# The row sums of the token norms from two rounded halves, and those of the second block one strip later

## What is computed

```python
def _rms_norm(x, g):
    xf = x.astype(jnp.float32)
    y = xf * lax.rsqrt(jnp.mean(xf * xf, axis=-1, keepdims=True) + EPS)
    return (y * g.astype(jnp.float32)).astype(x.dtype)
...
        h = h + mixed @ w_out[l]
        h = h + _cross_attention(_rms_norm(h, norm_x_g[l]), _rms_norm(mem, norm_mem_g[l]),
                                 xa_wq[l], xa_wk[l], xa_wv[l], xa_wo[l])
        h = h + jnp.square(jax.nn.relu(_rms_norm(h, norm_ff_g[l]) @ ff_w1[l])) @ ff_w2[l]
    return _rms_norm(h, final_norm_g)
...
        # second block, on that result
        h = rmsnorm(x, ln1_g[l])
        proj = h @ w_in[l]
        b_a, c_a, x_a, x_b, g_b, gate_a_logit, gate_b_logit = jnp.split(proj, SPLIT_POINTS, axis=-1)
        y_a = b_a * causal_depthwise_conv(c_a * x_a, conv_a_w[l])
        u_b = causal_depthwise_conv(x_b, conv_b_w[l], conv_b_b[l])
        y_b = rg_lru(u_b, lru_wa[l], lru_ba[l], lru_wx[l], lru_bx[l], lru_lambda[l])
...
        h = rmsnorm(x, ln2_g[l])
        x = x + (jax.nn.silu(h @ w_ffn_gate[l]) * (h @ w_ffn_up[l])) @ w_ffn_down[l]
```

## Time and profile before

| | |
|---|---|
| Time, median of 3 runs (lowest to highest) | 1694.38 us (1694.36 to 1695.56) |
| The profiled execution: time, span of the trace | 1695.03 us, 1693.2 us |
| Busy in the span: TensorE | 1660.7 us (98%), 7450 matmul records |
| VectorE, ScalarE, GpSimd | 894.1, 645.5, 823.7 us |
| Granted TensorE clock, mean | 0.995 of full |
| Plain fp32 matmul records of the token norms (L679 and L1165) | 8 and 2, 0.59 us each |
| Waits of TensorE for GpSimd's low parts (L570) | 6.9 us in 3 waits, one of them 6.2 us |

### The profile page before, as it was taken

The page is one execution under the profiler, slowest core; times in us unless marked ns, Lnnn a source line. Parts: engine busy times, 40 slices in busy tenths (PEclk is TensorE's granted clock), DMA queues, the critical chain, the costliest instruction groups (busy, mean ns, idle before and its releaser), DMA issues.

```text
span 1693.2 us, 21197 instructions
## 1 busy us (share of the span) xinstructions
PE 1660.7 (98%) x7450; PEld 1361.5 (80%) x7450; DVE 894.1 (53%) x1176; ACT 645.5 (38%) x827; POOL 823.7 (49%) x604
## 2 busy tenths in 40 slices
PE   7989999999999999999999999999999999999997
PEld 5868878888778888888888888888888888888886
DVE  7997896664357333344557676743333432232234
ACT  5534334443233221122345657563333431222222
POOL 4555245645225444444436656564444444444443
PEclk9999999999999999999999999999999999999999
DMA  6113222243112233223223333332233222222323
GB/s 238 62 63 100 87 66 97 88 150 99 62 63 89 98 99 99 94 92 99 99 87 114 110 101 119 103 105 93 99 99 99 88 99 99 97 90 98 99 99 100
DMA packets 48927, 167.04 MB, mean 99 GB/s; under 512 B 5285, under 2 KB 7461, under 8 KB 48618
## 3 DMA queue, kind: packets, MB, share of 16 engines
q1 hardware_dynamic: 44864, 158.51, 28.2%
q10 hardware_dynamic: 4010, 7.80, 1.3%
HBM read 164.18 MB, written 2.11 MB: 98 GB/s over the span
## 4 chain that ended last, share of the span: by engine, by line
PE 47%; issue 20%; POOL 14%; DVE 1%; DMA 0%; ACT 0%; POOLq 0%; DVEq 0%; SPq 0%
PE ps L651 16%; PE ps L653 16%; PE ps L652 16%; POOL m_w_lo L570 13%; DMA m_raw<-in_strips 0%; POOL m_QL L611 0%; DVE m_h L2584 0%; PE ps L910 0%; PE ps L912 0%; PE ps L911 0%; ACT m_w_hi L1253 0%; POOLq L587 0%; POOLq L585 0%; DVE ps L2170 0%; DVE m_s L2161 0%
## 5 line engine op out<-in xcount | busy, mean ns | idle before, releaser
L570 POOL TENSOR_TENSOR m_w_lo<-m_raw,m_w_hi 128x512 fp32r<-128x512 f32 x582 | 791.7, 1382 | 812.4 <-ACT m_w_hi L1253 812.2
L1253 ACT ACTIVATE m_w_hi<-m_raw 128x1024 fp32r<-128x1024 f32 x291 | 306.8, 1057 | 590.4 <-DMA m_raw<-in_strips 590.3
L651 PE MATMUL ps<-m_XH,m_w_hi 128*128 128x512 f32 x1096 | 437.6, 399 | 7.3 <-POOL m_w_lo L570 6.9
L653 PE MATMUL ps<-m_XH,m_w_lo 128*128 128x512 f32 x1096 | 427.7, 390 | 0.0
L652 PE MATMUL ps<-m_XL,m_w_hi 128*128 128x512 f32 x1000 | 390.0, 390 | 0.0
L651 PEld LDWEIGHTS ps<-m_XH,m_w_hi 128*128 128x128 f32 x1096 | 206.4, 188 | 57.7 <-POOL m_w_lo L570 9.8
L653 PEld LDWEIGHTS ps<-m_XH,m_w_lo 128*128 128x128 f32 x1096 | 206.1, 188 | 43.4
L652 PEld LDWEIGHTS ps<-m_XL,m_w_hi 128*128 128x128 f32 x1000 | 188.3, 188 | 41.9 <-issue 4.1
L651 PE MATMUL ps<-m_FH,m_w_hi 128*128 128x512 f32 (+1 forms) x438 | 169.3, 387 | 0.3 <-DVE m_FL L1791 0.3
L653 PE MATMUL ps<-m_FH,m_w_lo 128*128 128x512 f32 (+1 forms) x438 | 169.1, 386 | 0.0
L652 PE MATMUL ps<-m_FL,m_w_hi 128*128 128x512 f32 (+1 forms) x438 | 169.1, 386 | 0.0
(11 more groups left out here) (410 smaller groups left out, 2198.8 us busy)
## 6 DMA issues: line engine op xcount, KB each, us to landing
m_raw<-in_strips SPq DMA_DIRECT2D x294, 512.0 KB, 3.3
m_x_in<-in_x SPq DMA_DIRECT2D x4, 512.0 KB, 8.1
m_spread<-g_kept ACTq DMA_DIRECT2D x8, 256.0 KB, 3.3
m_x_res<-in_x ACTq DMA_DIRECT2D x1, 2048.0 KB, 9.2
m_memf<-in_mem SPq DMA_DIRECT2D x1, 1024.0 KB, 14.6
m_w<-in_w ACTq DMA_DIRECT2D x2, 512.0 KB, 8.6
m_decay<-in_decay ACTq DMA_DIRECT2D x1, 1024.0 KB, 11.8
out<-m_h SPq DMA_DIRECT2D x8, 128.0 KB, 1.7
```

The source lines that it names most:

```text
L570: nc.gpsimd.tensor_tensor(w_lo[:, c], raw[:, c], f(w_hi[:, c]), ALU.subtract).then_inc(lo_ready, 1)
L651: pe.matmul(dst, hi[:, c], xh, start=first, stop=False)
L653: return pe.matmul(dst, lo[:, c], xh, start=False, stop=last)
L1253: act.activation(w_hi[:, c], raw[:, c], ACT.Copy).then_inc(hi_ready, 1)
```

## The change

Every norm's row sum is now made from two rounded parts. VectorE splits the sum of squares into a high part (rounded to fp32r) and the rest, two instructions (`split`), where it only raised a semaphore before. TensorE multiplies a block of ones in fp32r by each part into one bank, two matmuls of 512 columns (`rows_sum`) in place of a plain fp32 one. The ones in fp32r lie where `tri[0]` was and are written once, in the first block, behind the use of the mask. The high and low part of `acc` lie in `s0` and `s1`, those of `e0` in `e1` and, in place, in `e0`. In the second block both row sums move from behind the strip w = 0 to behind the strip w = 1 of turn 0.

```diff
+        ones_r = at("ones_r", P, small + 256 + (NCOL + 2 * P) * 4, F32R)
+        acc_hi = at("acc_hi", T, small + 9760, F32R)
+        acc_lo = at("acc_lo", T, small + 11808, F32R)
+        e_hi = at("e_hi", T, 192 * KB + 5632, F32R)
+        e_lo = at("e_lo", T, 192 * KB + 3584, F32R)
...
             def norm(n):
                 pe.wait_ge(norm_sum, n)
-                pe.matmul(ps[:, 7, :], ones, acc[:], start=True, stop=True).then_inc(norm_all, 1)
+                rows_sum(7, acc_hi, acc_lo).then_inc(norm_all, 1)
+
+            def rows_sum(bank, hi, lo):
+
+                pe.matmul(ps[:, bank, :], ones_r[:], hi[:], start=True, stop=False)
+                return pe.matmul(ps[:, bank, :], ones_r[:], lo[:], start=False, stop=True)
...
-                        if first and w == 0:
+                        if first and w == 1:
                             norm(4)
-                            pe.matmul(ps[:, 6, :], ones, e0[:], start=True, stop=True).then_inc(norm_two, 1)
+                            pe.wait_ge(norm_sum, 5)
+                            rows_sum(6, e_hi, e_lo).then_inc(norm_two, 1)
...
                         if u == 0:
-                            norm(5)
+                            norm(6)
...
             def mlstm_sums():
 
                 ch.sync()
+                ch.add(dve.tensor_copy(ones_r[:], ones))
                 dve.wait_ge(m_sums, 4 * TT)
...
                 dve.wait_ge(summed, 8 * r + KT)
-                dve.sem_inc(norm_sum, 1)
+                split(acc_hi[:], acc_lo[:], acc[:], 1.0, norm_sum)
...
             dve.wait_ge(summed, 16 + KT)
+            split(acc_hi[:], acc_lo[:], acc[:], 1.0, norm_sum)
             dve.wait_ge(summed_two, KT)
-            dve.sem_inc(norm_sum, 1)
+            split(e_hi[:], e_lo[:], e0[:], 1.0, norm_sum)
             dve.wait_ge(norm_all, 5)
```

## The result

After the change the kernel takes **1698.85 us** (median of 19 runs, 1697.06 to 1701.19), against 1695.56 us for the kernel before in the same comparison (19 runs, 1694.36 to 1696.91). The ratio is 1.0020 with an interval of 1.0013 to 1.0026: 3.3 us slower, 0.2%, small but clear of noise by the interval, where 3.5 were forecast. The profiled execution took 1698.85 us, its span is 1697.1 us.

The account below looks back on a forecast made before the run. In the second block's turns the chain of VectorE and ScalarE was taken to lead, TensorE following without slack. A 4.84 us late chain less 1.34 us from rounded sums gave +3.5 us on 1694.38: 1697.9 us, range 1696.6 to 1700.0.

Parts of the forecast that it names:

- The rounded sum: Norms 2, 3 and 5 on TensorE's path: 0.45 us less each, 1.34 us gained, at least 1.20.
- The splits: VectorE's two instructions ahead of each sum, 1.2 to 3.2 us: hidden, 0; not hidden if the sum came at 875.00.
- Rival D: Splits come late at three norms, up to 0.9 us each, with GpSimd beside them: 1700.5 us; chance 2%.
- The copy of the ones: One 128x128 VectorE instruction in the first block, at most 1.3 us, covered by a 7.29 us wait: 0.
- The chain: VectorE and ScalarE's hand-offs from turn 0's moved sums start 4.84 us late (4.80 to 5.04); each later step shifts alike.
- The two waits: Turn 0: TensorE waits 3.4 us for strip S_IN + 4, then 2.7 us for the next turn's first strip; clock at 1.00.
- Rival A: TensorE's clock falls behind turn 0's new waits, 2 us each, first absorbed, second costing 0 to 2: 1698.9 us; chance 10%.
- Turn 1: Second block: turn 1 begins 4.84 us late, whatever TensorE saved in turn 0; less than 4 would refute the argument.
- The turns: Second block: turns stay 28.87 us, TensorE's own work 28.56; the 0.3 us are waits for the chain, with no catching up.
- rival B: The chain catches up in the turns, TensorE pays only the S_IN + 4 wait: +1.2 us, 1695.6 us; chance 8%.
- Rival C: Late sums cost nothing if S_IN + 4's high part is ready regardless: -2.2 us, 1692.1 us; chance 6%.
- The sum: Whole kernel: 4.84 late less 1.34 gained, +3.5 us, 3.4 to 3.9: 1697.9 us, 0.21% slower.

Follow-up runs that it names:

- r_first: The changed kernel with the second block's row sums put back behind the strip w = 0, rounded sums kept: 1695.34 us, ratio 1.0002.
- r_second_high: The changed kernel with ScalarE's high part of strip S_IN + 4 taken ahead of its two roots in turn 0: 1697.78 us, ratio 1.0018.
- r_second_defer: The changed kernel with the final norm's two VectorE steps and root made later in turn 0, off the way to `pX`: 1695.70 us, ratio 1.0001.
- the three kernels with the swap: Next turn's `pX` taken before the BH/BL split, in the kernel before, with rounded sums behind w = 0, and in the changed kernel: 0.9996, 0.9993, 1.0015.
- r_second_defer_swap_mg: The changed kernel plus deferred second norm, `pX` ahead of the BH/BL split, and the merge's fourth strip's high part earlier: 1694.43 us, ratio 0.9994.
- r_first_early: The changed kernel, sums back behind w = 0, with ScalarE taking the high part of each next turn's first strip one step earlier: 1697.87 us, 1.0017.
- r_first_swap: The changed kernel, sums back behind w = 0, with the next turn's `pX` taken ahead of the BH/BL split: ratio 0.9993.

## Why the prediction was right

**The rounded sum: right.** Forecast 0.45 us each, at least 0.40; measured 0.43 at norms 2 and 3, about 0.5 at norm 5 in `after` and 0.4 in `r_first`. Sum forecast 1.34, measured 0.86 + 0.51 = 1.37 in `after`, 1.25 in `r_first`.

**The splits: hidden at every norm**, as the median of the earlier trace rows had it. Rival D is out. The one split that met a low part beside it (1.66 us at 874.28) ended at 875.94, 4.1 us ahead of the sum. The sentence that it wouldn't be hidden at 875.00 is shown by `r_first`: 0.78 us of wait there.

**The copy of the ones** took 1.28 us, the upper end of its bound, and cost nothing: VectorE still waited 6.05 us for TensorE behind it. The cover was what counted.

**The chain: 4.84 us late, to the hundredth.** VectorE's first step came 6.11 us behind w = 0 (forecast 6.1), the second sum's wait of 0.24 us went, `pX` and the high part of S_IN + 4 are 4.85 and 4.84 late. Every step behind kept its length nearly.

**The two waits: in place, both smaller.** 3.15 us for 3.4, and 1.24 for 2.7. The first is short by 0.25, since TensorE reached it nearly 0.1 later and the low part came 0.16 earlier than worked out. The second is short by what the clock took in between, 1.63 us, less those 0.16. **This is the one statement on the mechanism that failed**: the granted clock was to stay at 1.00 behind both waits, and was 0.53 behind the first. The mistake was to take the wait of 2.41 us that had not lowered it for a guide to one of 3.4. The same trace has a shorter one, of 2.27 us, that did lower it; timeline of TensorE and the clock behind it, of the kernel before:

```profile
254.87 3.99 PE L845 MATMUL ps<-m_VX,m_W 128*128 128x129 f32 x20 [2.27 <-DVE m_acc L2076]
```

```profile
254.87:258.87 4.00, 4.00 (x21) 4.00 (x22) 1.84 (x3) 1.06 (x1) 2.06 (x2) 0.59 0.06 22
```

Rival A named the case, with 2 us behind the first wait that only eat into the second; that is what happened, and so the time didn't change. By the prediction's own sign ("if the clock falls, it is A") the case is A, and the 1698.85 us measured are A's 1698.9 and not the forecast's 1697.9. But A's number holds 1 us for its other half, a slow clock behind the second wait, which didn't come in `after`; the agreement with it is luck, as this section's last paragraph shows. `r_second_high` and `r_second_defer` did run into a low clock in front of turn 1, and lost 1.95 and 1.38 us between C and D, within A's range of 0 to 2.

**Turn 1: 4.74 us late** (forecast 4.84). **The turns: 28.88 us** (28.87): no catching up, so rival B is out, and the three kernels with the swap show why: the 0.3 us a turn are the chain's, and once they are gone TensorE's own pace is the limit. **Rival C** falls with the loss itself; `r_second_high` shows in addition that C's condition, a high part that is early, would not have been enough: turn 1 still began 3.33 us late.

**The sum**: 4.78 to D, less 1.37, is +3.4 us by the distances and +3.3 by the medians, against +3.5. The absolute time, 1698.85 for 1697.9, is 0.95 higher; the kernel before itself ran 1.2 higher in this comparison, at 1695.56 and not at 1694.38.

## What to carry to other kernels

When two engines hand work to each other without slack, ask when the first input of that chain comes, not how busy TensorE is: 0.45 us saved three times lost against an input that came 4.84 us late. Before a step is moved to where it can't stall the busiest engine, work out the chain behind it to the next place where that engine waits for the chain. And a gap in front of TensorE may cost more than its length, so look whether a second wait behind it covers the slow matmuls or none does, and don't take one execution's clock behind such a gap for what the next will show.

## What the runs showed of the hardware

**The granted clock** fell to its lower level behind waits that I had thought too short for it: 8 matmuls 0.43 us apart behind 2.98 us (3.15 by the starts) in `after`, 13 behind 4.0 in `r_second_high`, 8 behind 2.14 in `r_second_defer` and 2.12 in `r_second_defer_swap_mg`, a loss of 1.6 us for 8 (3.45 less 1.82) and 2.75 for 13 (5.70 from 903.38 to 909.08, less 2.95).

The length of the wait doesn't decide it, and the same instructions don't even decide it twice alike. All 13 traces have a wait of 2.3 us at about 255 us and one of 2.4 us at about 286, ahead of anything that the kernels differ in but the copy of the ones. Behind the first, 8 traces have a granted clock of 0.57 to 0.63 over 4 us and 5 have 1.00 (20 matmuls that take 2.47 us at 1.00 take 3.7 to 4.1 us in the eight). Behind the second, 10 have 1.00 and 3 (`r_first_early`, `r_first_swap`, `r_second_high`) fall to the lower level some six matmuls later; all three are among those that stayed at 1.00 behind the first. Timeline and clock of `r_second_high`, for the earlier trace rows:

```profile
286.44 0.47 PE L656 MATMUL ps<-m_QH,m_far_hi 128*128 128x512 f32 x1 [2.38 <-POOL m_QL L616]
```

```profile
286.40:289.00 2.60, 2.56 (x9) 2.08 (x10) 2.56 (x3) 1.06 (x1) 2.39 (x3) 0.78 0.24 96
```

So one trace can't promise that such a wait leaves the clock alone, and the prices above, too, are those of one execution each. What else decides it was not tried. The Trainium skill, "TensorE: Matmul & The Clock Gate", section "HAM oscillation — how this bites in real kernels", has idle gaps between groups of matmuls as the cause; the falls here agree, each behind such a gap, and the 1.00 behind others of 2.3 and 2.4 us shows that not each gap brings one.

**A rounding copy of 128x128** took 1.28 us on VectorE (287.85), three times the 0.43 of a rounding step of 128x512 elsewhere. GpSimd had begun a low part 0.1 us ahead of it, and a low part runs beside the longest splits too; timeline of GpSimd in `after`:

```profile
287.74 5.07 POOL L575 TENSOR_TENSOR m_w_lo<-m_raw,m_w_hi 128x512 fp32r<-128x512 f32 x4
```
